# Value products in two column halves and a new order of the second attention, in a two-block network on one core

## What is computed

```python
# first attention: window of 128, blocks of 128 queries see their own and the previous key block
scores = einsum("bnqkgd,bnjkd->bnkgqj", qb, kw) * scale          # 4 key heads, 4 query heads each
m = maximum(max(where(valid, scores, -inf), -1), sink)
p = exp(scores - m[..., None])
probs = p / (sum(p, -1) + exp(sink - m))[..., None]
out = einsum("bnkgqj,bnjkd->bnqkgd", probs, vw)
y_attn = out * silu(g_attn)
...
# second attention: each query takes the 128 best keys by an index score, causal
_, sel = top_k(score, topk)
logits = einsum('bqgrd,bqkgd->bqgrk', qg, kg) * scale            # 4 key heads, 4 query heads each
p = softmax(where(sel_ok, logits, -1e30))
o = einsum('bqgrk,bqkgd->bqgrd', p, vg)
return o @ w_out
```

## Time and profile before

| | |
|---|---|
| median of 3 runs | 1817.74 us (1811.52 to 1818.07) |
| profiled execution | 1816.34 us, its span 1814.5 us |
| mean granted TensorE clock | 0.976 of full |
| TensorE busy | 1708.3 us, 94% |
| VectorE busy | 1047.8 us, 58% |
| ScalarE busy | 737.9 us, 41% |
| value products L563, 136 records | 67.3 us busy |

### The profile page before, as it was taken

The page is one execution under the profiler, slowest core; times in us unless marked ns, Lnnn a source line. Parts: engine busy times, 40 slices in busy tenths (PEclk is TensorE's granted clock), DMA queues, the critical chain, the costliest instruction groups (busy, mean ns, idle before and its releaser), DMA issues.

```text
span 1814.5 us, 22668 instructions
## 1 busy us (share of the span) xinstructions
PE 1708.3 (94%) x7488; PEld 1324.0 (73%) x7488; DVE 1047.8 (58%) x2091; ACT 737.9 (41%) x1392; POOL 63.0 (3%) x43
## 2 busy tenths in 40 slices
PE   5999999999998997799899999998999899999999
PEld 3777667777876765337688888886888678888887
DVE  7787766666456698963655564366444543333334
ACT  4363766663343233783443322324223244332322
POOL 0020000000000063000000000000000000000000
PEclk9999999999998997999899999998999899999999
DMA  6342334433331121002255554252333232232333
GB/s 232 135 166 95 123 133 158 145 139 134 95 91 57 47 61 45 1 1 70 73 198 193 185 186 163 91 199 83 102 97 100 70 93 92 93 102 95 97 101 104
DMA packets 55812, 201.65 MB, mean 111 GB/s; under 512 B 6192, under 2 KB 6320, under 8 KB 55600
## 3 DMA queue, kind: packets, MB, share of 16 engines
q1 hardware_dynamic: 55728, 200.57, 33.1%
HBM read 198.44 MB, written 2.10 MB: 111 GB/s over the span
## 4 chain that ended last, share of the span: by engine, by line
PE 81%; DVE 11%; ACT 5%; issue 2%; POOL 0%; DMA 0%; DVEq 0%; ACTq 0%; POOLq 0%
PE bank L450 25%; PE bank L452 24%; PE bank L451 24%; PE bank L563 2%; DVE G L1390 1%; ACT SB L964 1%; DVE SB L1535 1%; PE bank L552 1%; DVE H_lo L1384 1%; DVE W_lo L1320 1%; ACT PT L978 1%; PE bank L533 1%; DVE SB L1892 1%; PE bank L660 1%; DVE WORK L1810 1%
## 5 line engine op out<-in xcount | busy, mean ns | idle before, releaser
L450 PE MATMUL bank<-H_hi,W_hi 128*128 128x512 f32 x1416 | 578.7, 409 | 22.0 <-DVE H_lo L1384 12.2
L451 PE MATMUL bank<-H_lo,W_hi 128*128 128x512 f32 x1416 | 556.8, 393 | 0.0
L452 PE MATMUL bank<-H_hi,W_lo 128*128 128x512 f32 x1416 | 556.5, 393 | 0.0
L1320 DVE TENSOR_TENSOR W_lo<-RAW,W_hi 128x512 fp32r<-128x512 f32 x538 | 351.4, 692 | 196.3 <-ACT W_hi L839 180.6
L839 ACT CAST W_hi<-RAW 128x512 fp32r<-128x512 f32 x538 | 313.0, 618 | 234.9 <-PE bank L452 211.6
L450 PEld LDWEIGHTS bank<-H_hi,W_hi 128*128 128x128 f32 x1416 | 268.1, 189 | 120.0 <-issue 44.3
L451 PEld LDWEIGHTS bank<-H_lo,W_hi 128*128 128x128 f32 x1416 | 269.2, 190 | 58.1 <-issue 7.0
L452 PEld LDWEIGHTS bank<-H_hi,W_lo 128*128 128x128 f32 x1416 | 268.7, 190 | 58.0
L450 PE MATMUL bank<-A_hi,W_hi 128*128 128x512 f32 x352 | 137.0, 389 | 0.0
L452 PE MATMUL bank<-A_hi,W_lo 128*128 128x512 f32 x352 | 136.9, 389 | 0.0
L451 PE MATMUL bank<-A_lo,W_hi 128*128 128x512 f32 x352 | 136.9, 389 | 0.0
(11 more groups left out here) (255 smaller groups left out, 1915.9 us busy)
## 6 DMA issues: line engine op xcount, KB each, us to landing
RAW<-weights SPq DMA_DIRECT2D x269, 512.0 KB, 3.6
AW<-ada SPq DMA_DIRECT2D x100, 512.0 KB, 3.6
X<-x_t SPq DMA_DIRECT2D x4, 512.0 KB, 5.6
y_t<-X SPq DMA_DIRECT2D x8, 256.0 KB, 2.0
LW<-lru_w SPq DMA_DIRECT2D x1, 1024.0 KB, 12.9
CROW<-crow SPq DMA_DIRECT2D x1, 512.0 KB, 10.9
ROPE<-rope SPq DMA_DIRECT2D x1, 512.0 KB, 13.7
CS<-constants SPq DMA_DIRECT2D x1, 386.5 KB, 8.1
```

The costliest lines, as they stand in the source:

```text
L450: pe.matmul(dst, wh, ch(hi, k), start=(k == 0), stop=False)
L451: pe.matmul(dst, wh, ch(lo, k), start=False, stop=False)
L452: mm = pe.matmul(dst, wl, ch(hi, k), start=False, stop=(k == chunks - 1))
L1320: dve.tensor_tensor(W_lo[:, w], RAW[:, c:c + HALF], W_hi[:, w], ALU.subtract).then_inc(lo_done, 1)
```

## The change

1. `pv`: for each key block there are two matmuls instead of one, each with the same 64 columns of V and 256 moving columns. The first writes rows 0 to 63 of bank 6, the second rows 64 to 127, both in columns 0 to 255. `turn_probs` puts the heads in the order 0, 2, 1, 3, so that the two halves come out in the layout that YT had.
2. `heads_out` and its two semaphores go. `y_gate` and, in the second attention, `heads_hi` and `y_out` read bank 6 directly. `pv(s)` waits for `y_gate(s - 1)` or `y_out(s - 1)`, where it waited for `heads_out`.
3. The second attention's lists for one step s become:
   - TensorE: turn_probs(s), qk(s + 2, 0 to 2), pv(s), qk(s + 2, 3)
   - ScalarE: heads_hi(s - 1), exps(s + 1), probs_out(s)
   - VectorE: score(s + 1, 3), minus_max(s + 1), normalise(s), y_out(s - 1), select, score(s + 2, 0 to 2)

```diff
             def pv(s):
...
-                if s:
-                    pe.wait_ge(yt_out, s)
+                if 0 < s <= 16:
+                    pe.wait_ge(yy_done, s)
+                elif s > 16:
+                    pe.wait_ge(y_lo_done, s)
                 for c, kb in enumerate(keys):
                     pe.wait_ge(pt_out, PT_COUNT[s] + c + 1)
                     at_col = kb * 2 * P + V_ORDER[s // 16][g] * HD
-                    mm = pe.matmul(ps[6][0:HD, :], V[:, at_col:at_col + HD],
-                                   ch(PT, c), start=(c == 0), stop=(c == len(keys) - 1))
+                    for odd in range(2):
+                        mm = pe.matmul(ps[6][odd * HD:(odd + 1) * HD, 0:2 * P], V[:, at_col:at_col + HD],
+                                       PT[:, c * S + odd * 2 * P:c * S + (odd + 1) * 2 * P],
+                                       start=(c == 0), stop=(c == len(keys) - 1))
...
+            qk(17, (3,))
             for s in range(16, 32):
-                if s < 31:
-                    qk(s + 1, (3,))
-                if s < 30:
-                    qk(s + 2, (0,))
                 turn_probs(s)
                 if s < 30:
-                    qk(s + 2, (1, 2))
+                    qk(s + 2, (0, 1, 2))
                 pv(s)
+                if s < 30:
+                    qk(s + 2, (3,))
...
             for s in range(16, 32):
                 if s > 16:
-                    heads_out(s - 1)
                     heads_hi(s - 1)
-                probs_out(s)
                 if s < 31:
                     exps(s + 1)
-            heads_out(31)
+                probs_out(s)
             heads_hi(31)
...
             def y_gate(s):
-                dve.wait_ge(yt_out, s + 1)
+                dve.wait_ge(pv_mm, s + 1)
...
-                dve.tensor_tensor(yt, yt, y_region(GA, s), ALU.mult).then_inc(yy_done, 1)
+                heads = ps[6][:, 0:2 * P].rearrange("p (k t) -> p k t", k=2)
+                dve.tensor_tensor(yt, heads, y_region(GA, s), ALU.mult).then_inc(yy_done, 1)
...
             for s in range(16, 32):
-                normalise(s)
                 if s < 31:
                     score(s + 1, 3)
                     if s + 1 == 19:
                         query_roots(2)
                     minus_max(s + 1)
+                normalise(s)
+                if s > 16:
+                    y_out(s - 1)
                 if s < 26:
                     select(ROUNDS_S[s - 16])
                 if s < 30:
                     for h in range(3):
                         score(s + 2, h)
-                if s > 16:
-                    y_out(s - 1)
```

More of the change, by code:

```diff
@@ L311, in build @@
         crow_in, crow_done = sem("crow_in"), sem("crow_done")
-        dve_chain, act_chain, pool_chain = sem("dve_chain"), sem("act_chain"), sem("pool_chain")
+        dve_chain, pool_chain = sem("dve_chain"), sem("pool_chain")
         prm_done = sem("prm_done")
@@ L336, in build @@
         exp_done, norm_done = sem("exp_done"), sem("norm_done")
-        pt_mm, pt_out, pv_mm, yt_out = sem("pt_mm"), sem("pt_out"), sem("pv_mm"), sem("yt_out")
+        pt_mm, pt_out, pv_mm = sem("pt_mm"), sem("pt_out"), sem("pv_mm")
         yy_done, y_hi_done, y_lo_done = sem("yy_done"), sem("y_hi_done"), sem("y_lo_done")
@@ L551, in turn_probs @@
                         src = (s % 2) * 4 * width + h * w + c * P
-                        mm = pe.transpose(ps[banks[c]][:, h * P:(h + 1) * P], SB[:, src:src + P], cs("ident"))
+                        to = (h % 2 * 2 + h // 2) * P
+                        mm = pe.transpose(ps[banks[c]][:, to:to + P], SB[:, src:src + P], cs("ident"))
                     mm.then_inc(pt_mm, 1)
@@ L829, in _ @@
         def _(act):
-            chain = Tally(act_chain)
             def split_hi(tile, halves=range(2)):
@@ L978, in probs_out @@
                     act.copy(ch(PT, c), ps[banks[c]][:]).then_inc(pt_out, 1)
[L980 to L989, removed]
             def y_region(t, s):
@@ L997, in heads_hi @@
                     act.wait_ge(yy_done, s + 1)
+                    heads = YT[:, :]
                 else:
-                    act.wait_ge(yt_out, s + 1)
-                    act.wait_ge(act_chain, chain.n)
-                act.copy(y_region(YA_hi, s), YT[:, :].rearrange("p (k t) -> p k t", k=2)).then_inc(y_hi_done, 1)
+                    act.wait_ge(pv_mm, s + 1)
+                    heads = ps[6][:, 0:2 * P]
+                act.copy(y_region(YA_hi, s), heads.rearrange("p (k t) -> p k t", k=2)).then_inc(y_hi_done, 1)
             fn_count = [0]
@@ L1061, in _ @@
                     fill_hi(s, 0)
-            heads_out(15)
             heads_hi(15)
@@ L1542, in y_gate @@
             def y_gate(s):
-                dve.wait_ge(yt_out, s + 1)
+                dve.wait_ge(pv_mm, s + 1)
                 yt = YT[:, :].rearrange("p (k t) -> p k t", k=2)
+                if s:
+                    dve.wait_ge(y_lo_done, s)
                 if s % 4 == 0:
                     dve.wait_ge(ga_done, GA_NEED[s // 4])
-                dve.tensor_tensor(yt, yt, y_region(GA, s), ALU.mult).then_inc(yy_done, 1)
+                heads = ps[6][:, 0:2 * P].rearrange("p (k t) -> p k t", k=2)
+                dve.tensor_tensor(yt, heads, y_region(GA, s), ALU.mult).then_inc(yy_done, 1)
             def y_out(s):
-                yt = YT[:, :].rearrange("p (k t) -> p k t", k=2)
+                heads = (YT[:, :] if s < 16 else ps[6][:, 0:2 * P]).rearrange("p (k t) -> p k t", k=2)
                 dve.wait_ge(y_hi_done, s + 1)
-                dve.tensor_tensor(y_region(YA_lo if s < 16 else YA2_lo, s), yt, y_region(YA_hi, s), ALU.subtract).then_inc(y_lo_done, 1)
+                dve.tensor_tensor(y_region(YA_lo if s < 16 else YA2_lo, s), heads, y_region(YA_hi, s),
+                                  ALU.subtract).then_inc(y_lo_done, 1)
             GA_NEED = [2, 4, 6, 8]
```

## The result

The changed kernel takes 1828.16 us (median of 5 runs, 1826.95 to 1833.98) against 1817.74 before; the ratio is 1.0073, 95% interval 1.0050 to 1.0095. It is slower by about 10 us. The forecast was no change, 1817, with a chance of 0.20 for slower; the time lies inside the range of 1804 to 1831, but on a side that was held unlikely. The profiled execution took 1826.97 us.

What follows compares the result with a forecast made beforehand. TensorE, busy 94% of the span, was taken as the bound; in the second attention, a loop between three engines. First attention -8.4, second +8 (+1.2 order, +7 clock), sum -0.4: 1817 us, range 1804 to 1831.

Steps and rivals of the forecast that it cites:

- Value product, first attention: First attention: the two column halves run at once, saving 0.74 us a product at two key blocks; sum -8.4 us.
- the early steps: First attention, steps 0 to 4: product savings become longer waits at the next scores; 2.0 of 2.9 us left out.
- rival 4: Both attentions: the halves don't overlap, first gains 0 to 1 us, second's loops get longer; 1828 at full clock; chance 0.06.
- Heads read from the bank: Both attentions: removes two ScalarE copies a step; holding bank 6 until its readers finish costs 0.
- The condition that I named, y_out late: Bank 6: if y_out came late, the product and all behind it on TensorE would wait up to 0.4 us.
- The new order at the clock of before: Second attention: product, fourth scores, score, minimum, normalise and transposes form one loop without overlap; sum +1.2 us.
- The end: Second attention, last reciprocals to output projection: exponentials and copies run beside other work, 10.8 us for 18.9, -8.1.
- Rival 1: Second attention: ScalarE is the loop, 6.6 us for 7.95 at four key blocks; total 1796; chance 0.07.
- The clock: Second attention: TensorE's gaps drop its clock, 1.5 us a fall; five falls count, +7 us, between 0 and +20.
- rival 3: Second attention: the clock falls in nearly every step, fourteen falls of 1.5 us; total 1832; chance 0.12.
- these steps: Second attention, four steps with one key block: loop 4.2 us at full clock, 5.5 at half; +1.5, between 0 and +4.
- for two key blocks: Second attention: VectorE with its selections is the bound, 25.2 us stay; +0.4 for one step without two selections.

Runs made afterwards that it cites:

- e8: Kernel before with each value product split into two matmuls of 256 columns, both into rows 0 to 63 of the bank; 1816.75 us, ratio 0.9998.
- e1: Changed kernel with the second attention's three old lists put back; column halves and heads read from the bank stay; 1817.37 us, ratio 1.0005.
- e7: Changed kernel with one to three added matmuls on constants a step behind the fourth head's scores in the second attention; 1811.95 us, ratio 0.9982.
- e3: Changed kernel with VectorE taking normalise(s) ahead of score(s + 1, 3) and minus_max(s + 1) again; 1805.88 us, ratio 0.9941.
- e4: Changed kernel with TensorE taking the fourth head's scores qk(s + 2, 3) ahead of pv(s); 1805.58 us, ratio 0.9936.
- e10: Changed kernel with the list edits of e3 and e4 together; 1798.93 us, ratio 0.9902.
- e9: e1 with VectorE's y_out(s - 1) moved right behind minus_max(s + 1), ahead of the selection; 1806.59 us, ratio 0.9941.
- e11: e9 with one added matmul of 512 columns of constants behind each product of the second attention; 1804.11 us, ratio 0.9930.
- e12: e10 with one added matmul of 512 columns of constants behind each product of the second attention; 1799.67 us, ratio 0.9907.

## Why the prediction was wrong

**Value product, first attention: right.** -8.4 was forecast. From the product of step 0 (196.05 before, 195.77 after) to the load of the positions, which waits for the last copies (415.45 and 405.55), it is -9.6. Per product with two key blocks 0.84 is saved, not the 0.74 taken; the 0.1 that I took off for a late start of the second half isn't there. In steps 0 to 3 nothing was gained: step 3's product starts at 241.59 and 241.60. I had put 0.9 on the early steps. e8 shows that the overlap is the reason (rival 4 falls).

In a sentence by itself: worked out from the efficiency that the Trainium skill, "TensorE: Matmul & The Clock Gate", Part 3, gives for three column tiles, an estimate, it would have been 0.64 a product; the runs show 0.84.

**Heads read from the bank: right here, only by the place of y_out.** The cost of 0 holds in the new order. The condition that I named, y_out late, is what e1 has, and there it cost 11.5 us over the stage, not a part of 0.4 a step: what I priced was the subtraction, and what stood ahead of it in VectorE's list is what is waited for.

**The new order at the clock of before: right.** Loops of 7.6, 8.4 and 9.5 us were forecast, 7.7, 8.46 and 9.6 measured in e7; that fourth scores behind the product and normalise behind the score together make the loop is shown by e3 and e4, each of which removes one link and the loss. The end took 12.2 us where 10.8 was forecast, and 13.5 in e7 at full clock, with its added matmuls; that is 2.7 of the 3.2 by which e7's +4.4 lies above the +1.2 of the sum. Rival 1 falls: no step with four key blocks ran at 6.6 us with the fourth scores and the normalise where the change put them.

**The clock: the step that failed.** "I take five that count, +7." By the loop sums the stage should have been +1.2 at the clock of before; it was +22.9, so this term was some 22 and not 7 (e7 puts it at 18.4, with its added matmuls), and the stage lies outside its own bounds of -1 to +20. That is rival 3, to which I gave 0.12. Three things were missed.

First, I counted falls of 3 us each from full clock, and took the fall of the earlier trace rows for the only one. The stage begins at the lower level, in both kernels, behind some 13 us in which TensorE is nearly idle; and the kernel before has another fall at 738, where the gap before was 0.98 us. Windows of the kernel before (two), of the changed kernel ahead of the stage, and of e10:

```profile
707.00:720.50 13.50, 2.97 (x12) 2.38 (x12) 7.80 (x30) 2.02 (x8) 6.97 (x3) 0.50 0.00 0
738.00:740.50 2.50, 2.50 (x6) 0.72 (x6) 2.09 (x10) 2.48 (x10) 0.00 (x0) 0.50 0.02 7
697.50:710.03 12.53, 2.47 (x10) 1.89 (x10) 7.32 (x31) 2.05 (x9) 6.97 (x3) 0.50 0.00 1
719.00:737.00 18.00, 17.98 (x60) 9.67 (x61) 15.60 (x66) 9.70 (x31) 0.00 (x0) 0.50 0.00 0
```

In the kernel before the clock rose at 727; in the changed kernel it never rose in the first four steps: 0.50 over all 26.2 us, where the same steps took 19.7 before at a mean clock of 0.76. The loop doesn't make this level by itself: e3, e4, e9 and e10, where it is open, have 0.50 over these steps too, and take 18.6 to 22.1 us. What costs is the lower clock and the loop together. Second, my sum had 5.5 a step at the lower level and +4 as its upper bound for these steps; 6.6 and +6.5 were measured. Third, for two key blocks I took VectorE's work as the bound. At full clock it nearly is (25.9 in e7); at a mean clock of 0.71 TensorE's part of the loop outgrows it, and 25.2 us became 32.5.

In sentences by themselves: the Trainium skill, "TensorE: Matmul & The Clock Gate", Part 1, says that activity lifts the clock. I had this as a remark against the change, and not in the sum. The four runs with filled gaps agree with it (0.68 to 0.83 in the first four steps, where the same kernels without the added matmuls have 0.50). e10 agrees less: its TensorE was busy 17.98 of 18.00 us from 719 to 737, at 0.50 throughout.

**Net.** -9 for the first attention was offset, and more, by the second. The total stayed in the range because that took in most of rival 3, and because the rest gained 12.2 us and not 8.4; with the second attention outside its own bounds, that is partly luck. What stays open is when the clock falls and when it returns: which of the loop's idle stretches drops it, and why it stays at 0.50 for so long in e10, no run here shows.

## What to carry to other kernels

When items of in-order lists are exchanged, write down for each engine what now stands ahead of each item, and follow the circle: here two harmless moves (a score behind the product, a normalise behind the score) closed a loop through TensorE and VectorE in which nothing overlaps, and undoing either one won 22 us. Reading a result straight from its bank saves the copy but ties the next product to the reader's place in its list. On a path where TensorE waits in every step, its time is better reckoned at 1.2 GHz as well, and the clock at the start of the stage is read from the trace first: added matmuls in the gap were worth 18 us of the stage in the loop, 2 in the old order (e11), and nothing in the fastest order (e12).

## What was unexpected of the hardware

Float32 matmuls of 64 weight columns that write partitions 0 to 63 and 64 to 127 of one bank from different moving columns overlapped wholly: 1.02 us for eight passes against 1.87. And the clock didn't follow TensorE's busy time alone: in the changed kernel's first four steps it stayed at its lower level with TensorE busy 18.7 of 26.2 us, in e7 at three key blocks it never fell with 30.3 of 32.3, but in e10 it stayed at the lower level for 18 us in which TensorE was busy all the time.
